# One kernel for two transformer blocks: product tiles completed in pairs around the norms that join the blocks, the two norms made in one step, and one count read of TensorE moved

## The chip, the cores and the metric

The kernel runs on 1 core of one Trainium2 chip. The metric is the time of one execution on the device, in microseconds. TensorE (PE in the profile) multiplies into eight PSUM banks of 128x512 fp32, and loads the stationary operand beside that (PEld); VectorE (DVE), ScalarE (ACT), GpSimd (POOL) and SyncE (SP, which here only issues transfers) work beside it, each through its own instructions in order. Engines wait for each other by semaphores that count up.

## What is computed

Two blocks run one after the other on 512 tokens of width 1024, all in fp32. Only their joint matters here: the end of the first block, the first block's last norm, the second block's first norm, and the product behind it.

```python
def rmsnorm(x, g):
    y = xf * lax.rsqrt(jnp.mean(xf * xf, axis=-1, keepdims=True) + EPS)
    return y.astype(x.dtype) * g
# end of first_block
    x = x + hier_moe(h, w_grp[i], w_exp[i], w1[i], w3[i], w2[i])
    h = rmsnorm(x, g_ple[i])
    x = x + jax.nn.sigmoid(h @ w_pg[i]) * (p[i] @ w_ple[i])
    return rmsnorm(x, g_final)
# start of second_block
    h = rms_norm(x, norm_mix[layer])
    proj = h @ w_in[layer]
```

EPS is 1e-6. The residual x of the second block is the output of the norm by g_final.

## The kernel before

**Products.** Every large product is made of fp32 operands that are each cut into a high part (a rounded fp32r copy, made by ACT: `split_hi` for weights, `act_hi` for activations) and the rest (made by DVE: `split_lo`, `act_lo`). A product of 512 contraction rows by 512 columns is a *chunk*; for each of its 4 token tiles, `tile_passes` issues 4 x 3 matmuls (high x high, high x low, low x high; 12 in all) into the PSUM bank of that tile, `gb[j]`. A *unit* is 512 output columns and has two chunks (kc 0 and 1), so it has 8 tiles of 12 matmuls. Weights of a chunk go through `w_stage[s]`, `w_hi[s]` and `w_lo[s]`, s = 0 or 1 by turns; a slot can be refilled when the last tile that reads it is done (`pe_tiles`).

**The end of block one.** The gate product `g_pg` (h @ w_pg) has two units of 8 tiles. In both, PE takes kc 0 for token tiles 0 to 3, then kc 1 for 0 to 3, so a bank is complete only from the fifth tile on. As a bank completes, ACT makes the sigmoid out of it (`gate_rows`, `sg_t`), and DVE multiplies and adds it into x (`embed`, lines 1717 and 1719; semaphore `x_ple`). The second unit is `second_unit(g_pg)`.

**The two norms.** When a token tile of x is whole, ACT squares and sums its row (`sum_squares`, line 793) and takes the root (line 795); DVE inverts that and scales x by it and g_final in place (`scale_rows`, lines 1283 and 1287). Then the same again for the second block's norm: sum, root, inverse, and the scaled rows go to `xn`. PE turns the scaled rows (`turn_rows`, line 2016, 8 transposes of 128x128 to a token tile), ACT and DVE cut them into `act_hi` and `act_lo` (lines 810 and 1274), and `norm_and_product(4, g_sv)` runs the first product of block two, one unit of 8 tiles. Weights' cuts for `g_sv` stand among these steps (`mid=`).

**Behind it.** A small product with 16 weight columns (line 2447, `low_hi`, `low_lo`) and then `g_gv`. GpSimd clears `low_f` once x is whole, and only then does SP load it, and behind it on the same queue the weights of `g_gv`.

**The count read.** Block one's experts run in rounds of 64 slots. After the first round each engine reads the fullest expert's count (`value_load(most)`; for PE line 2403) and branches over the further rounds (line 2404). With these inputs no further round runs. Behind the branch PE takes the embedding product p @ w_ple (`embedding_tile`, line 2421).

## Time and profile before

| | us |
|---|---|
| runs of the kernel before (3), median | 1835.64 |
| lowest and highest | 1835.12, 1837.38 |
| the profiled execution, whole | 1835.13 |
| its span, first to last instruction | 1833.5 |
| PE busy | 1769.7 |
| DVE, ACT, POOL busy | 796.7, 587.2, 66.3 |

All times of single instructions count from the start of the span. The whole time is 1.6 us more than the span. PE is busy 97% of the span, so what can be won lies in the few places where it stands idle or at half clock, and the mean busy share doesn't show where these are; the chain of waits and the timeline do.

### The profile page before, as it was taken

The page shows a single profiled execution, that of the slowest core. Times are in us where ns is not written, and L with a number is a line of the kernel's source. Part 1 is how long each engine was busy: PE and PEld are TensorE (multiplying, and loading weights), DVE is VectorE, ACT ScalarE, POOL GpSimd, SP SyncE. Part 2 cuts the span into 40 slices and gives each one's busy share as a digit, 9 for nine tenths or more (in the row PEclk, how much of TensorE's full clock was granted, in tenths as well). Part 3 has the DMA queues.
Part 4 walks back from the last instruction along what each step waited for, and adds up shares of the span by engine and source line. Part 5 has one row for each costly group of instructions (what it writes and reads, how often), then busy time and mean ns, then how long its engine had stood idle before and what let it go on. Part 6 is the DMA issues. An engine that isn't in the chain of part 4 may idle for free.

```text
span 1833.5 us, 21542 instructions
## 1 busy us (share of the span) xinstructions
PE 1769.7 (97%) x8428; PEld 1284.1 (70%) x8428; DVE 796.7 (43%) x1104; ACT 587.2 (32%) x729; POOL 66.3 (4%) x123
## 2 busy tenths in 40 slices
PE   6999999979999999999979999999999989999998
PEld 5887887754444454544758777788868878888886
DVE  5323338453333333333553445666656444323432
ACT  5333443222121212122443433344442333213422
POOL 2000000000000000000000012300000000000000
PEclk9999999989999999999989999999999999999999
DMA  5222223947999999999222222223243322233222
GB/s 195 92 92 92 69 69 92 359 167 308 420 421 422 421 417 410 418 409 353 74 64 82 83 93 70 69 76 109 92 139 111 107 69 92 93 108 97 92 92 80
DMA packets 90447, 326.20 MB, mean 178 GB/s; under 512 B 8569, under 2 KB 9089, under 8 KB 65809
## 3 DMA queue, kind: packets, MB, share of 16 engines
q1 hardware_dynamic: 88640, 320.08, 46.6%
q0 software_dynamic: 1744, 5.26, 0.8%
q8 instruction: 43, 0.70, 0.2%
q14 instruction: 20, 0.16, 0.0%
HBM read 319.03 MB, written 6.29 MB: 177 GB/s over the span
## 4 chain that ended last, share of the span: by engine, by line
PE 94%; DVE 3%; ACT 2%; DMA 1%; issue 1%; SPq 0%; DVEq 0%; ACTq 0%
PE bank L1991 59%; PE bank L2303 12%; PE bank L2316 6%; PE bank L2220 3%; PE bank L2263 3%; PE bank L2016 2%; PE bank L2529 2%; ACT xg L957 1%; PE bank L2421 1%; PE bank L2467 1%; PE bank L2488 1%; DMA w_stage<-in_w_in 1%; DVE xn L1287 0%; PE bank L2566 0%; DVE act_lo L1274 0%
## 5 line engine op out<-in xcount | busy, mean ns | idle before, releaser
L1991 PE MATMUL bank<-act_hi,w_hi 128*128 128x512 f32 x992 | 392.0, 395 | 2.0 <-DVE act_lo L1274 2.0
L1259 DVE TENSOR_TENSOR w_lo<-w_stage,w_hi 128x2048 fp32r<-128x2048 f32 x99 | 226.5, 2288 | 378.0 <-ACT w_hi L777 378.0
L1991 PE MATMUL bank<-act_lo,w_hi 128*128 128x512 f32 x992 | 387.8, 391 | 0.0
L1991 PE MATMUL bank<-act_hi,w_lo 128*128 128x512 f32 x992 | 387.8, 391 | 0.0
L777 ACT ACTIVATE w_hi<-w_stage 128x2048 fp32r<-128x2048 f32 x99 | 189.7, 1916 | 415.7 <-PE bank L1991 412.2
L1991 PEld LDWEIGHTS bank<-act_hi,w_hi 128*128 128x128 f32 x992 | 187.4, 189 | 43.9 <-issue 5.9
L2303 PE MATMUL bank<-ring,xgT 128*64 128x512 f32 x992 | 215.7, 592 | 0.7 <-ACT xgT L961 0.7
L1991 PEld LDWEIGHTS bank<-act_hi,w_lo 128*128 128x128 f32 x992 | 187.2, 189 | 39.4
L1991 PEld LDWEIGHTS bank<-act_lo,w_hi 128*128 128x128 f32 x992 | 187.4, 189 | 38.3 <-issue 0.5
L2303 PEld LDWEIGHTS bank<-ring,xgT 128*64 128x64 f32 x992 | 71.1, 137 | 141.6 <-issue 140.6
L1991 PE MATMUL bank<-w_hi,act_hi 128*128 128x512 f32 x288 | 114.2, 397 | 6.0 <-DVE act_lo L1274 5.1
L2316 PE MATMUL bank<-ring,gatedT 128*64 128x512 f32 x512 | 113.4, 595 | 0.8 <-DVE gatedT L1619 0.8
L1991 PE MATMUL bank<-w_hi,act_lo 128*128 128x512 f32 x288 | 113.1, 393 | 0.0
L1991 PE MATMUL bank<-w_lo,act_hi 128*128 128x512 f32 x288 | 113.0, 393 | 0.0
L1991 PE MATMUL bank<-w_hi,hid_hi 128*128 128x512 f32 x256 | 99.6, 389 | 0.0
L1991 PE MATMUL bank<-w_lo,hid_hi 128*128 128x512 f32 x256 | 99.6, 389 | 0.0
L1991 PE MATMUL bank<-w_hi,hid_lo 128*128 128x512 f32 x256 | 99.6, 389 | 0.0
L957 ACT ACTIVATE xg<-bank 128x512 f32<-128x512 f32 x32 | 34.2, 1074 | 191.2 <-PE bank L2220 191.2
L2316 PEld LDWEIGHTS bank<-ring,gatedT 128*64 128x64 f32 x512 | 35.4, 137 | 67.5 <-issue 66.5
L1588 DVE TENSOR_TENSOR x_tm<-x_tm,bank 128x512 f32<-128x512 f32 x128 | 78.0, 680 | 0.0
L1610 DVE TENSOR_TENSOR gated<-gated,bank 128x512 f32<-128x512 f32 x16 | 11.0, 688 | 151.1 <-PE bank L2303 151.1
L1626 DVE SCALAR_TENSOR_TENSOR y_lo_sb<-bank,slot_gate,y_hi_sb 128x512 fp32r<-128x512 f32 x32 | 23.3, 750 | 122.0 <-ACT y_hi_sb L989 121.9
(364 smaller groups left out, 2076.1 us busy)
## 6 DMA issues: line engine op xcount, KB each, us to landing
ring<-in_w SPq DMA_DIRECT2D x188, 1024.0 KB, 11.4
w_stage<-in_w_in SPq DMA_DIRECT2D x46, 1024.0 KB, 5.1
w_stage<-in_w_ff SPq DMA_DIRECT2D x32, 1024.0 KB, 5.2
w_stage<-in_w_out SPq DMA_DIRECT2D x8, 1024.0 KB, 5.1
extra<-in_w SPq DMA_DIRECT2D x4, 1024.0 KB, 7.8
branch_gates<-gate_out POOLq DMA_DIRECT2D x16, 256.0 KB, 2.4
w_stage<-in_w_proj_gla SPq DMA_DIRECT2D x4, 1024.0 KB, 10.0
w_stage<-in_w_pg SPq DMA_DIRECT2D x3, 1024.0 KB, 5.8
```

Of the source, the lines that this page charges most:

```text
L777: act.activation(w_hi[s][:, 0:ktiles, :], w_stage[s][:, 0:ktiles, :], ACT.Copy)\
L957: act.activation(xg_by_row[:, b * (P // 2):(b + 1) * (P // 2), :], mb[b][:, :].rearrange("s (q k) -> s q k", k=KT), ACT.Copy).then_inc(xg_ ...
L1259: dve.tensor_tensor(w_lo[s][:, 0:ktiles, :], w_stage[s][:, 0:ktiles, :], w_hi[s][:, 0:ktiles, :].bitcast(F32), ALU.subtract).then_inc(w_lo ...
L1588: dve.tensor_tensor(xt, xt, bank[:, :], ALU.add).then_inc(moe_added, 1)
L1626: dve.scalar_tensor_tensor(y_lo_sb[:, half], gb[1 + b][:, :], slot_gate[:, col(i)], y_hi_sb[:, half].bitcast(F32), ALU.mult, ALU.subtract)\
L1991: ins = pe.matmul(gb[j][:, :], left, right, start=(kc == 0 and k == 0 and n_pass == 0), stop=(kc == g.chunks - 1 and k == g.ktiles - 1 and ...
L2016: return pe.transpose(dst, src, ident[0:rows, 0:rows])
L2220: return pe.matmul(mb[b][:, :], sel[:, t, :], part[:, t, b * 512:(b + 1) * 512], start=(part is xn_hi and t == 0), stop=(part is xn_lo and ...
L2263: ins = pe.matmul(bank[:, :], selT[:, t * P:(t + 1) * P], part[:, half], start=(part is y_hi_sb), stop=(part is y_lo_sb))
L2303: ins = pe.matmul(dst[mine, :], xgT[:, 4 * kh + k, mine], weights[:, k, :], start=(kh == 0 and k == 0), stop=(kh == 1 and k == 3), skip_gr ...
L2316: return pe.matmul(gb[1 + nh][mine, :], gatedT[:, k, mine], ring[8 + 2 * (k // 2) + q][:, 2 * (k % 2) + nh, :], start=(k == 0), stop=(k == ...
L2529: ins = pe.matmul(mb[t][:, h * P:(h + 1) * P], left[:, h, cols], right[:, h, cols], start=True, stop=True, skip_group_check=True)
```

## The change

1. **Order of tiles.** The second unit of `g_pg` and the unit of `g_sv` take their tiles as PAIRED says: (tile, kc) = 0/0, 1/0, 0/1, 1/1, 2/0, 3/0, 2/1, 3/1. Banks 0 and 1 are complete after the fourth tile. The transposes of token tiles 0 and 1 stand ahead of the last two tiles of `g_pg`, those of 2 and 3 ahead of the fourth and fifth tile of `g_sv`. `split_hi` has a mode `paired` that waits for the sixth tile of a unit and not for all.
2. **The norms.** With m the mean of x squared and q the mean of (x g_final) squared, the two roots in a row are 1/sqrt(q + EPS m + EPS squared). DVE makes `xg_tm` = x g_final by half rows (`final_gain`), ACT sums the squares of x and of xg by half rows, GpSimd makes the joint root of a token tile in three steps (`both_rstd`), and DVE makes xn in one step (`both_norms`). The residual x = xg / sqrt(m + EPS) is made later by ACT (4 instructions of 128x1024), with a root for all tiles from GpSimd.
3. **ACT's table.** A dummy sigmoid stands ahead of the gates; no square root is taken at the joint any more.
4. **The count read.** PE's `value_load` stands in `last_pair` between `turn_gated` and the wait for `gatedT_out`; the branch stays where it was.

```diff
         def rows_count(n, t):
-            if n in (3, 4):
-                return 3 * NT + ((1, 2, 4, 6) if n == 3 else (3, 5, 7, 8))[t]
             return n * NT + t + 1
+        PAIRED = ((0, 0), (1, 0), (0, 1), (1, 1), (2, 0), (3, 0), (2, 1), (3, 1))
...
-            pool.wait_ge(x_ple, 2 * NT)
+            pool.wait_ge(n_sd, rows_count(3, NT - 1))
+            own.did(pool.tensor_scalar(both_var[:, :], ms_x[:, 0, :], EPS, EPS * EPS, ALU.mult, ALU.add))
+            own.settle()
+            own.did(pool.tensor_tensor(both_var[:, :], both_var[:, :], ms_xg[:, 0, :], ALU.add))
+            for t in range(NT):
+                mine = slice(t, t + 1)
+                pool.wait_ge(n_sd, rows_count(4, t))
+                own.settle()
+                own.did(pool.tensor_scalar(both_var[:, mine], ms_x[:, 1, mine], EPS, both_var[:, mine],
+                                           ALU.mult, ALU.add))
+                own.settle()
+                own.did(pool.tensor_tensor(both_var[:, mine], both_var[:, mine], ms_xg[:, 1, mine], ALU.add))
+                own.settle()
+                pool.tensor_tensor(both_rstd[:, mine], both_var[:, mine], root_power[:, mine], ALU.pow)\
+                    .then_inc(pg_scale, 1)
+            own.did(pool.tensor_tensor(row_rstd[:, :], ms_x[:, 0, :], ms_x[:, 1, :], ALU.add))
+            own.settle()
+            own.did(pool.tensor_scalar(row_rstd[:, :], row_rstd[:, :], EPS, None, ALU.add))
+            own.settle()
+            pool.tensor_tensor(row_rstd[:, :], row_rstd[:, :], root_power[:, :], ALU.pow).then_inc(pg_scale, 1)
+            pool.wait_ge(x_ple, 3 * NT)
             pool.memset(low_f[:, :, :], 0.0).then_inc(low_pad, 1)
...
-                if not isinstance(c, int) or c >= 2:
+                if paired:
+                    act.wait_ge(pe_tiles, (c - 1) * 4 + 2)
+                elif not isinstance(c, int) or c >= 2:
...
+            act.activation(table_col[:, :], one_col[:, :], ACT.Sigmoid)
+            def gate_rows(u, j, before):
+                act.wait_ge(pe_tiles, (g_pg.chunk0 + 2 * u) * 4 + before)
+                if u:
+                    act.wait_ge(x_ple, j + 1)
+                act.activation(sg_t[j][:, :], gb[j][:, :], ACT.Sigmoid, scale=rstd[:, j:j + 1]).then_inc(out_act, 1)
+            def row_squares(rows, u, t, sums, junk):
+                half = slice(u * 512, (u + 1) * 512)
+                return act.activation(junk[:, t, half], rows[:, t, half], ACT.Square, scale=float(D) ** -0.5,
+                                      accum_out=sums[:, u, t:t + 1])
+            def squares_x(u, t):
+                act.wait_ge(x_ple, NT + 2 * t + 1 if u else t + 1)
+                row_squares(x, u, t, ms_x, sq_tm)
+            def squares_xg(u, t):
+                if u:
+                    act.wait_ge(x_ple, NT + 2 * t + 2)
+                else:
+                    act.wait_ge(n_xn, rows_count(3, t))
+                row_squares(xg_tm, u, t, ms_xg, xn_at[4]).then_inc(n_sd, 1)
+            def rows_high(t):
+                for b in range(2):
+                    q = 2 * t + b
+                    act.wait_ge(n_tp, turned_before(4) + q + 1)
+                    act.activation(act_hi[:, 4 * b:4 * b + 4, t * P:(t + 1) * P],
+                                   mb[q % 4][:, :].rearrange("p (k t) -> p k t", k=4), ACT.Copy).then_inc(n_hi, 1)
             split_hi(g_pg.chunk0 + 2, 0)
             act.wait_ge(pg_scale, 1)
-            gate_rows(0)
+            for j in range(4):
+                gate_rows(0, j, 4 + j + 1)
             split_hi(g_pg.chunk0 + 3, 1)
-            gate_rows(1)
-            def end_of_block(t):
-                act.wait_ge(x_ple, NT + t + 1)
-                sum_squares(3, t)
-            def next_rows(t):
-                if t + 1 < NT:
-                    end_of_block(t + 1)
-                act.wait_ge(n_xn, rows_count(3, t))
-            end_of_block(0)
-            norm(4, next_rows, mid=lambda: split_hi(g_sv.chunk0, 0))
+            for t in range(NT):
+                squares_x(0, t)
+                squares_xg(0, t)
+            for t in range(2):
+                gate_rows(1, t, 3 + t)
+                squares_x(1, t)
+                squares_xg(1, t)
+            split_hi(g_sv.chunk0, 0, paired=True)
+            rows_high(0)
+            gate_rows(1, 2, 7)
+            rows_high(1)
+            gate_rows(1, 3, 8)
             split_hi(g_sv.chunk0 + 1, 1)
+            for t in range(2, NT):
+                squares_x(1, t)
+                squares_xg(1, t)
+            rows_high(2)
+            rows_high(3)
+            act.wait_ge(pg_scale, 2 + NT)
+            for t in range(NT):
+                own.did(act.activation(x[:, t, :], xg_tm[:, t, :], ACT.Copy, scale=row_rstd[:, t:t + 1]))
...
+            def final_gain(u, j):
+                half = slice(u * 512, (u + 1) * 512)
+                if u == j == 0:
+                    dve.wait_ge(gain_in, 48)
+                dve.wait_ge(x_ple, NT + 2 * j + 1 if u else j + 1)
+                dve.tensor_tensor(xg_tm[:, j, half], x[:, j, half], gain[:, half], ALU.mult)\
+                    .then_inc(x_ple if u else n_xn, 1)
+            def both_norms(t):
+                if t == 0:
+                    dve.wait_ge(gain_4_in, 16)
+                dve.wait_ge(pg_scale, t + 2)
+                dve.scalar_tensor_tensor(xn_at[4][:, t, :], xg_tm[:, t, :], both_rstd[:, t:t + 1], gain_4[:, :],
+                                         ALU.mult, ALU.mult).then_inc(n_xn, 1)
+            def rows_low(t):
+                for b in range(2):
+                    q = 2 * t + b
+                    dve.wait_ge(n_hi, turned_before(4) + q + 1)
+                    rest(act_lo[:, 4 * b:4 * b + 4, t * P:(t + 1) * P],
+                         mb[q % 4][:, :].rearrange("p (k t) -> p k t", k=4),
+                         act_hi[:, 4 * b:4 * b + 4, t * P:(t + 1) * P]).then_inc(n_lo, 1)
             for j in range(NT):
                 embed(0, j)
+                final_gain(0, j)
             split_lo(g_pg.chunk0 + 3, 1)
-            def end_of_block(t):
-                if t + 1 < NT:
-                    embed(1, t + 1)
-                scale_rows(3, t)
-            embed(1, 0)
-            norm(4, end_of_block, mid=lambda: split_lo(g_sv.chunk0, 0))
+            for t in range(2):
+                embed(1, t)
+                final_gain(1, t)
+            both_norms(0)
+            both_norms(1)
+            split_lo(g_sv.chunk0, 0)
+            rows_low(0)
+            rows_low(1)
+            embed(1, 2)
             split_lo(g_sv.chunk0 + 1, 1)
+            final_gain(1, 2)
+            embed(1, 3)
+            final_gain(1, 3)
+            both_norms(2)
+            both_norms(3)
+            rows_low(2)
+            rows_low(3)
...
+            def paired_unit(g, u, before={}):
+                for n, (j, kc) in enumerate(PAIRED):
+                    if n in before:
+                        before[n]()
+                    tile_passes(g, g.chunk0 + 2 * u + kc, g.tile0 + 4 * u + j, kc, kc, j, fm=False)
...
                     turn_gated(n)
+                    if r is None:
+                        counts.append(pe.value_load(most[0:1, 0:1], min_val=0, max_val=T))
                     pe.wait_ge(gatedT_out, n + 1)
...
+            counts = []
             experts_pe(None)
-            fullest = pe.value_load(most[0:1, 0:1], min_val=0, max_val=T)
+            fullest = counts[0]
...
-            second_unit(g_pg)
-            norm_and_product(4, g_sv)
+            paired_unit(g_pg, 1, {6: lambda: turn_rows(4, 0), 7: lambda: turn_rows(4, 1)})
+            def rows_split(q):
+                pe.wait_ge(n_lo, turned_before(4) + q + 1)
+            def turned_and_split(t, q):
+                turn_rows(4, t)
+                rows_split(q)
+            paired_unit(g_sv, 0, {0: lambda: rows_split(0), 1: lambda: rows_split(2), 2: lambda: rows_split(3),
+                                  3: lambda: turn_rows(4, 2), 4: lambda: turned_and_split(3, 4),
+                                  5: lambda: rows_split(6), 6: lambda: rows_split(7)})
```

What the order of instructions shows at three places (names carry buffer numbers; `xn` is the scaled rows, `bank4` and up are the banks for transposes).

PE, the joint, before: the last matmuls of `g_pg`'s second unit, then the transposes of token tiles 0 and 1 and the first tile of `g_sv`.

```order
L1991 MATMUL bank3<-w_hi1_86,act_hi_81 128x512
L1991 MATMUL bank3<-w_lo1_88,act_hi_81 128x512
L1991 MATMUL bank3<-w_hi1_86,act_lo_82 128x512
L2016 MATMUL bank4<-ident_50,xn_2_91 128x128 x4
L2016 MATMUL bank5<-ident_50,xn_2_91 128x128 x4
L2016 MATMUL bank6<-ident_50,xn_2_91 128x128 x4
L2016 MATMUL bank7<-ident_50,xn_2_91 128x128 x4
L1991 MATMUL bank0<-w_hi0_85,act_hi_81 128x512
```

And now, behind the sixth tile of that unit:

```order
L2082 MATMUL bank3<-w_hi0_86,act_hi_82 128x512
L2082 MATMUL bank3<-w_lo0_88,act_hi_82 128x512
L2082 MATMUL bank3<-w_hi0_86,act_lo_83 128x512
L2107 MATMUL bank4<-ident_50,xn_2_92 128x128 x4
L2107 MATMUL bank5<-ident_50,xn_2_92 128x128 x4
L2082 MATMUL bank2<-w_hi1_87,act_hi_82 128x512
L2082 MATMUL bank2<-w_lo1_89,act_hi_82 128x512
```

The first transposes moved from behind the unit to ahead of its last two tiles (bank 2 and bank 3 with `w_hi1`).

DVE, the joint, before: adds into x, the two norms in turn, and the weight cut of `g_sv`'s first chunk.

```order
L1717 TENSOR_TENSOR ple_tm<-ple_tm,sg_t_172 128x512
L1719 TENSOR_TENSOR x_tm<-x_tm,ple_tm 128x512
L1283 RECIPROCAL rstd<-rstd 128x1
L1287 SCALAR_TENSOR_TENSOR x_tm<-x_tm,rstd,gain 128x1024
L1717 TENSOR_TENSOR ple_tm<-ple_tm,sg_t_173 128x512
L1719 TENSOR_TENSOR x_tm<-x_tm,ple_tm 128x512
L1283 RECIPROCAL rstd<-rstd 128x1
L1287 SCALAR_TENSOR_TENSOR x_tm<-x_tm,rstd,gain 128x1024
L1283 RECIPROCAL rstd<-rstd 128x1
L1287 SCALAR_TENSOR_TENSOR xn_91<-x_tm,rstd,gain_94 128x1024
```

And now, from the add of token tile 1 to that of token tile 3:

```order
L1778 TENSOR_TENSOR x_tm<-x_tm,ple_tm 128x512
L1786 TENSOR_TENSOR xg_tm<-x_tm,gain 128x512
L1794 SCALAR_TENSOR_TENSOR xn_92<-xg_tm,row_sums,gain_95 128x1024 x2
L1318 TENSOR_TENSOR w_lo_88<-w_stage_84,w_hi_86 128x2048
L1333 TENSOR_TENSOR act_lo<-bank,act_hi 128x4x128 x4
L1776 TENSOR_TENSOR ple_tm<-ple_tm,sg_t_175 128x512
L1778 TENSOR_TENSOR x_tm<-x_tm,ple_tm 128x512
L1318 TENSOR_TENSOR w_lo_89<-w_stage_85,w_hi_87 128x2048
L1786 TENSOR_TENSOR xg_tm<-x_tm,gain 128x512
L1776 TENSOR_TENSOR ple_tm<-ple_tm,sg_t_176 128x512
```

Tiles 0 and 1 are normed, the first weight cut and their `act_lo` are done before tile 2 is added; the second weight cut now stands between the add of tile 2 and its product with g_final.

PE, the end of the experts, before: the last spread matmuls, the count read and the branch.

```order
L2263 MATMUL bank<-y_hi_sb,selT 128x512
L2263 MATMUL bank<-y_lo_sb,selT 128x512
L2403 TENSOR_LOAD most
L2403 ISA x2
L2404 COMPARE_AND_BRANCH
```

And now, where the count is read:

```order
L2107 MATMUL bank<-ident,gated 128x128 x4
L2475 TENSOR_LOAD most
L2475 ISA x2
L2414 MATMUL bank<-ring_128,gatedT 64x512
L2414 MATMUL bank<-ring_129,gatedT 64x512
```

The read stands some 48 matmuls earlier; only the compare and branch is left behind the spreads.

## Rows read from the trace of the kernel before

**Rows 1.** The page, busy time, share of the span and instructions of PE and others.

```profile
PE 1769.7 (97%) x8428; PEld 1284.1 (70%) x8428; DVE 796.7 (43%) x1104; ACT 587.2 (32%) x729; POOL 66.3 (4%) x123
```

**Rows 2.** Stretches: length, busy PE, PEld, DVE, ACT, POOL; granted clock, DMA share, GB/s.

```profile
884.00:886.00 2.00, 2.00 (x7) 1.53 (x6) 2.00 (x3) 0.60 (x1) 0.00 (x0) 0.50 0.00 0
899.00:943.00 44.00, 43.98 (x196) 36.12 (x194) 16.43 (x17) 16.95 (x22) 1.29 (x2) 1.00 0.28 96
943.00:960.00 17.00, 4.32 (x17) 3.52 (x18) 13.27 (x19) 15.26 (x28) 0.95 (x1) 0.57 0.08 9
1326.00:1328.00 2.00, 2.00 (x10) 1.77 (x11) 1.93 (x4) 2.00 (x5) 0.00 (x0) 1.00 0.00 0
```

**Rows 3.** Chain of waits in order of time: start us, us, what.

```profile
899.43 43.56 PE bank L1991 x192
...
963.95 0.87 PE bank L2016 x8
...
984.80 5.44 PE bank L2447 x24
```

**Rows 4.** Timeline of PE at the joint: start, us, instruction, idle before.

```profile
942.59 0.39 PE L1991 MATMUL bank<-w_hi,act_lo 128*128 128x512 f32 x1
952.10 1.97 PE L2016 MATMUL bank<-ident,xn 128*128 128x128 f32 x8 [9.12 <-DVE xn L1287]
...
959.62 0.80 PE L1991 MATMUL bank<-w_hi,act_hi 128*128 128x512 f32 x1 [1.43 <-DVE act_lo L1274]
```

**Rows 5.** PE's sequencer, lines 2403 and 2404: duration ns, start us.

```profile
L2403 PEldq TENSOR_LOAD <-most x1: 488/488/488, 878.4 to 878.4; - x1
L2404 PEldq COMPARE_BRANCH  x1: 3671/3671/3671, 879.3 to 879.3; - x1
```

**Rows 6.** Timeline of PE after two other idle stretches.

```profile
883.11 0.47 PE L2421 MATMUL bank<-ple_hi,pT_hi 128*128 128x512 f32 x1 [2.51 <-DVE x_tm L1588]
...
884.23 0.63 PE L2421 MATMUL bank<-ple_lo,pT_hi 128*128 128x512 f32 x1
...
886.79 0.63 PE L2421 MATMUL bank<-ple_lo,pT_hi 128*128 128x512 f32 x1
...
1325.92 4.37 PE L2544 MATMUL bank<-gv_tm,gkend_tm 128*128 128x256 f32 x19 [1.71 <-ACT gkend_tm L1175]
```

**Rows 7.** Timeline of ACT around the second unit of g_pg.

```profile
903.93 1.06 ACT L1036 ACTIVATE sq_tm<-x_tm 128x1024 f32<-128x1024 f32 x1
...
921.26 0.69 ACT L1045 ACTIVATE sg_t<-bank,rstd 128x512 f32<-128x512 f32 x1 [2.03 <-PE bank L1991]
921.84 1.91 ACT L777 ACTIVATE w_hi<-w_stage 128x2048 fp32r<-128x2048 f32 x1
...
943.02 0.69 ACT L1045 ACTIVATE sg_t<-bank,rstd 128x512 f32<-128x512 f32 x1 [2.03 <-PE bank L1991]
...
953.88 1.06 ACT L810 ACTIVATE act_hi<-bank 128x512 fp32r<-128x512 f32 x2
```

**Rows 8.** Timeline of DVE, the same stretch.

```profile
921.98 0.69 DVE L1717 TENSOR_TENSOR ple_tm<-ple_tm,sg_t 128x512 f32<-128x512 f32 x1 [1.30 <-ACT sg_t L1045]
...
923.79 2.29 DVE L1259 TENSOR_TENSOR w_lo<-w_stage,w_hi 128x2048 fp32r<-128x2048 f32 x1 [0.39 <-ACT w_hi L777]
...
950.76 1.28 DVE L1287 SCALAR_TENSOR_TENSOR xn<-x_tm,rstd,gain 128x1024 f32<-128x1024 f32 x1
...
958.29 1.28 DVE L1274 TENSOR_TENSOR act_lo<-bank,act_hi 128x512 fp32r<-128x512 f32 x2
```

**Rows 9.** Timeline of POOL: the root of norm 2.

```profile
906.21 0.24 POOL L725 TENSOR_SCALAR ssq<-ssq 128x4 f32<-128x4 f32 x1 [650.35 <-ACT sq_tm L1036]
906.54 1.05 POOL L727 TENSOR_TENSOR rstd<-ssq,root_power 128x4 f32<-128x4 f32 x1
```

**Rows 10.** Instructions of POOL's line 744: ns min/median/max, first and last start.

```profile
L744 POOL TENSOR_SCALAR_AFFINE_SELECT sb_w<-sb_w x32: 287/541/1207, 1078.7 to 1186.7; 128x128 f32<-128x128 f32 x32
```

**Rows 11.** DMA issues from 900 to 1000 us: KB each, median us to landing.

```profile
w_stage<-in_w_in SPq DMA_DIRECT2D x6, 1024.0 KB, 5.0
```

More of the change, by code:

```diff
@@ L281, in two_blocks @@
         gain_2 = at("gain_2", F + 0, [P, D])
+        xg_tm = at("xg_tm", F + 8, [P, NT, D])
         pg_stage = at("pg_stage", F + 4, [P, 4, 512])
@@ L1037, in _ @@
                                accum_out=ssq[:, t:t + 1]).then_inc(n_sd, 1)
-            def gate_rows(u):
-                for j in range(4):
-                    act.wait_ge(pe_tiles, (g_pg.chunk0 + 2 * u + 1) * 4 + j + 1)
-                    if u:
-                        act.wait_ge(x_ple, j + 1)
-                    act.activation(sg_t[j][:, :], gb[j][:, :], ACT.Sigmoid, scale=rstd[:, j:j + 1]).then_inc(out_act, 1)
+            act.activation(table_col[:, :], one_col[:, :], ACT.Sigmoid)
[4 more added lines that the diff above has]
+                act.activation(sg_t[j][:, :], gb[j][:, :], ACT.Sigmoid, scale=rstd[:, j:j + 1]).then_inc(out_act, 1)
@@ L1067, in _, with unit @@
+            act.wait_ge(pg_scale, 2 + NT)
+            for t in range(NT):
+                own.did(act.activation(x[:, t, :], xg_tm[:, t, :], ACT.Copy, scale=row_rstd[:, t:t + 1]))
             act.wait_ge(low_in, 32)
             act.activation(low_hi[:, :, :], low_f[:, :, :], ACT.Copy).then_inc(low_split, 1)
-            def unit(c, put, next_two=True):
-                split_hi(c + 2, 0)
+            def unit(c, put, next_two=True, paired=False):
+                split_hi(c + 2, 0, paired=paired)
@@ L1075, in unit @@
                     split_hi(c + 3, 1)
-            unit(g_sv.chunk0, evac_f(sbv, ACT.Copy))
+            own.settle()
+            unit(g_sv.chunk0, evac_f(sbv, ACT.Copy), paired=True)
             act.wait_ge(low_z, 1)
```

6 lines of the change are left out of this document (5 added, 1 removed).

## The prediction

> **What bounds the kernel now.** I read the page first: PE is busy for 1769.7 us, 97% of the span [rows 1]. So only places where PE stands idle or runs at half clock can give time back. The stretches show where: from 899 to 943 us, the gate product, PE is full and the granted clock is 1.00; from 943 to 960 us PE is busy for 4.32 of 17 us at a mean clock of 0.57 [rows 2]. The timeline of PE shows the same place: its last matmul of the gate product ends at 942.98, the first transposes start at 952.10 after 9.12 us idle, and the product of block two starts at 959.62 [rows 4]. The chain of waits says what the stretch costs: the next product of PE, line 2447, starts at 984.80, and what had to be done between is 96 matmuls and 4 turned token tiles. At full clock a matmul takes 43.56/192 = 0.227 us and a turned tile 0.87 us [rows 3], so the work is 96 x 0.227 + 4 x 0.87 = 25.3 us, out of 984.80 - 942.98 = 41.8. The joint loses 16.5 us; that is the ceiling of what parts 1 to 3 of the change can bring.
>
> A second, smaller gap lies ahead of the embedding product: PE idle for 2.51 us before 883.11, then matmuls of 0.63 us instead of 0.39; the first of these is at 884.23 and the seventh at 886.79, so 0.43 us apart instead of 0.227 [rows 6]. The granted clock there was 0.50, which is 1.2 GHz [rows 2]. With the one that the clock's fall met half way I count 8 slow matmuls: the stretch costs 8 x 0.2 = 1.6 us.
>
> **The change, part by part.** I keep the times of the trace before, and put the shift from the count read on at the end. A tile is 12 matmuls, 2.72 us. A gate starts on ACT 0.04 us after its tile; the last did at 943.02, so the k-th tile of the second unit frees its gate at 943.02 - (16 - k) x 2.72, counting the first unit's eight tiles as 1 to 8.
>
> *First unit and the weights behind it.* The gain product adds a DVE step of 0.69 us to each token tile. The last gate is at 921.26 [rows 7]; the two steps of its add follow from 921.98 on [rows 8], to 923.40, and the gain product to 924.1; the weight cut behind it moves from 923.79 [rows 8] to about 924.1 and ends at 926.4 instead of 926.1. In the new order PE wants it two tiles sooner, for tile 11, at about 926.5. It fits with 0.1 us left, and I cost it at nothing; if it is late, it is late by tenths.
>
> *Squares.* The 8 half squares of the first unit's columns are ACT's while PE works. For one I estimate 1.06 us less 0.43 for half the columns (the 2048-column copy takes 1.91, the 1024-column square 1.06 [rows 7]), so 0.63: 5 us from 923.8, done ahead of the first gate at 929.4. They are hidden.
>
> *Token tiles 0 and 1.* Bank 0 is complete at tile 11: gate 929.42, add done 931.55, gain product 932.3, its squares 932.95, and gate 1 only then (932.95, not 932.14, since ACT takes its work in order). Gain product 1 ends at 935.8, its squares at 936.5. The root on GpSimd is three steps: 0.24, about 0.24, and 1.05 for the power [rows 9], with gaps of 0.1: 1.8 us. Root 0 is there at 934.8, root 1 at 938.3. DVE's joint norm of tile 0 takes 1.28 us (the step of the same form [rows 8]): 935.8 to 937.1. PE wants it at 937.4. Norm 1 ends at 939.6, wanted at 937.4 + 0.87 + 2.72 = 941.0. No stall.
>
> *Weights and low parts of g_sv.* Its first high cut starts when tile 14 is done, 937.6, and takes 1.91; the low cut 939.6 to 941.9; `act_lo` of token tile 0 to 943.1 [rows 7, 8]. PE wants all that at 942.98 + 2 x 0.87 - 0.2 = 944.5. The second high cut follows the last gate (944.76): 945.35 to 947.3, the low cut to 949.6, wanted two tiles in, at 950.0. Both fit, the second with 0.4 us left.
>
> *Token tiles 2 and 3.* Here is the one stall that I expect. DVE stands at the second weight cut until 949.6; behind it are the gain product of tile 2 (950.2), whose squares end at 950.85. Root 2 is there at 952.65 if GpSimd takes 1.8 us, and norm 2 at 953.95. PE wants it after the third tile of g_sv, at 944.55 + 3 x 2.72 = 952.7: 1.25 us of stall. GpSimd's price is the term that the trace does not show: its rows for the power were measured beside an idle DVE. For a form that GpSimd ran 32 times beside a busy DVE the row has 287 ns at least, 541 in the middle and 1207 at most [rows 10]. That bounds what a held step adds: 0 or 0.92 us each, so the stall is 1.25 to 4.0 us. During root 2 DVE runs four steps of two SBUF operands nearly without a gap, so I take the middle row, 0.25 us for each of three steps: a stall of 2.0. Root 3 is wanted 3.6 us after root 2's norm is taken, and ready in time.
>
> The Trainium skill (GPSIMD Engine Reference, Key points) says that GpSimd shares its SBUF interfaces with VectorE and contends with its instructions of two SBUF inputs; embed and the gain product are of that kind. The page gives no price; by it the stall would lie above 1.25, as in my sum and, further, in the rival of the held steps.
>
> *Behind the product.* GpSimd clears low_f now behind all its roots, at about 957.7 (before: as soon as x was whole), and SP's transfers of g_gv's weights stand behind that clearing: issue near 959.5, landed 5.0 us later [rows 11], cut by ACT and DVE by 969.5. PE wants them behind line 2447, at 970.2 + 5.44 = 975.7. The four scalings that make x (about 1.1 us each, estimated from the 1.06 of the 1024-column square) end at 964 to 965, low_hi and low_lo by 967.5, wanted at 970.2. All hidden, with 2.7 us left at the least; the old cover was longer.
>
> *Sum of the joint.* 4 x 0.87 + 96 x 0.227 + 2.0 = 27.3 us in place of 41.8: 14.5 to 14.6 us won. The clock: an idle stretch of 1.71 us was followed by 1.00 [rows 2, 6], one of 2.51 by 0.50. I take it that 2.0 us does not lower it; if it does, it costs a slow stretch like that one, 1.6 us.
>
> *Count read.* The load starts at 878.4 and the branch at 879.3: 0.9 us, and then the branch takes 3.67 [rows 5], which is why PE waits until 883.1. The new place is ahead of a wait for a copy on DVE in which PE is idle anyway, so the 0.9 us is hidden there, by a margin of a few tenths. The branch starts 0.9 earlier and the idle stretch shrinks from 2.51 to 1.6 us, below the 1.71 after which the clock held; then the slow stretch behind it is gone too, 1.6 us. From there on every start is PE's (the copies and cuts of that stage wait for it), so both reach the end: 2.5 us.
>
> The Trainium skill (Runtime: NRT & Kernel Launch, Instruction fetch mechanics) says that a taken branch to a target outside the fetched pages stalls for a transfer of the page. By that rule the stall moves with the branch, which agrees with my sum and speaks against the rival in which the read brings nothing.
>
> Sum: 14.6 + 2.5 = 17.1 us. From the profiled execution's 1835.13 that gives 1818.0; this execution lies 0.5 us below the median of the runs shown and at their lower end, so the median may come out some tenths higher.
>
> **Rivals.**
> - *A shorter stall, or none,* is inside the forecast: without any the time would be 1816.0.
> - *GpSimd's steps are held hard.* At the top row of 1207 ns the stall at token tile 2 is 4.0 us, and the clock then falls for one stretch: 2.0 + 1.6 more, 1821.6. For it: DVE is dense exactly there. Against: the middle row is less than half of the top.
> - *The count read brings nothing.* If the branch waits until PE has run its queue empty (880.6), it ends where it did, the idle stretch and the half clock stay: 1835.13 - 14.6 = 1820.5. For it: the branch ends 2.4 us after the queue is empty, a figure that could be its own. Against: its row starts at 879.3, behind the load, and the load alone stands between it and the last matmul issued.
> - *Another operand is late at several tiles*, the two weight cuts with 0.1 and 0.4 us left: each 0.1 us more on ACT or DVE goes straight to PE. At 1 to 2 us for each cut and with the held roots the time is 1823 to 1827.
> - *Slower than before:* the first turn stalls PE, the clock falls to 1.2 GHz and does not come back until the product ends, since transposes and short waits stand between its tiles. Each tile would cost 12 x 0.2 = 2.4 us more; ten tiles 24 us: 1842. It decides from 7 slow tiles on. Against: the clock that was 0.50 at 884 to 886 was 1.00 all through 899 to 943 [rows 2], though transposes stand between the embedding's tiles too.
>
> **How the numbers follow.** Forecast 1818.0 (its own range 1816 to 1820): 0.58. Held roots: 0.17. Count read worth nothing: 0.12. Late operands: 0.09. Slower: 0.02; no effect, the gain eaten by waits that I do not see: 0.02. The range reaches from 1815.5 (no stall, less the scatter of half a microsecond) to 1823.5, which takes in held steps or a worthless count read, each alone, nearly both together (1824.1), and the smaller half of the late operands. A measurement here can tell 0.2%, 3.7 us, from no change. All cases but the last two are faster by more than that: faster 0.96, same 0.02, slower 0.02.
>
> **What would show it.** PE idle between the first transposes and line 2447 of 1 to 2.5 us in one piece, ahead of the turn of token tile 2; granted clock 1.00 over that stretch; from the last tile of the first gate unit to line 2447's start 21.8 + 27.3 = 49 us instead of 63.6. GpSimd's three steps by their rows: 1.8 us in all or 2.5. PE's idle before the embedding product 1.6 us and its matmuls 0.39. Wrong would be the step on which a stall stands ahead of tile 11, of g_sv's first or third tile, or of line 2447.

## The result and the profile after

| | before | after |
|---|---|---|
| median of 4 runs each, us | 1836.29 | 1819.05 |
| lowest and highest | 1835.12, 1837.38 | 1818.27, 1820.32 |
| the profiled execution | 1835.13 | 1818.27 |
| its span | 1833.5 | 1816.5 |

The ratio is 0.9907, with a 95% interval of 0.9890 to 0.9924: 17.2 us faster, where 17.1 were forecast. Below, a kernel is compared by four stretches between starts of PE's pieces in the chain of waits: **A** from the last down product to the embedding product, **B** from there to the gate product's second half by line 2082 (1991 before), **C** from there to the small product of line 2557 (2447 before), which holds the joint, and **D** from there to the end of the span. What lies ahead of A isn't touched by any edit, except that the moved read now stands at its end.

The page of the changed kernel, parts 1 and 2, says only that PE has 4.8 us less busy time than before [rows 1], which fits some 5 us of matmuls and transposes at half clock that are gone from B and C, and GpSimd 9 us more:

```profile
span 1816.5 us, 21572 instructions
PE 1764.9 (97%) x8428; PEld 1280.5 (70%) x8428; DVE 796.5 (44%) x1100; ACT 589.4 (32%) x741; POOL 75.7 (4%) x140
```

The chain of waits of the changed kernel, from stretch A to the end of C (start, duration, what):

```profile
869.70 7.11 PE bank L2414 x32
...
882.48 5.71 PE bank L2522 x24
...
897.23 38.12 PE bank L2082 x168
935.35 0.87 PE bank L2107 x8
936.23 2.77 PE bank L2082 x12
939.00 0.87 PE bank L2107 x8
939.87 2.75 PE bank L2082 x12
...
942.64 0.02 ACT sg_t L1073
942.67 0.56 issue
943.23 1.92 ACT w_hi L805
945.15 0.02 issue
945.17 2.29 DVE w_lo L1318
947.46 0.61 DVE xg_tm L1786
...
948.10 0.73 ACT xn L1077 x2
...
948.92 0.61 POOL row_sums L743
...
950.82 1.29 DVE xn L1794
...
952.16 1.09 PE bank L2107 x8
...
956.90 10.89 PE bank L2082 x48
967.79 5.44 PE bank L2557 x24
```

PE's tiles run through: 168 matmuls without a break, the transposes of token tiles 0 and 1 between tiles. The chain leaves PE once, from 942.6 on, through ACT's gate and second weight cut, DVE's second weight cut, the gain product behind it, the squares, the root and the norm of token tile 2. That is the path on which the prediction put the stall. The timeline of PE gives its size and that of the idle stretch ahead of the embedding product:

```profile
882.48 0.47 PE L2522 MATMUL bank<-ple_hi,pT_hi 128*128 128x512 f32 x1 [1.83 <-DVE x_tm L1647]
952.16 1.09 PE L2107 MATMUL bank<-ident,xn 128*128 128x128 f32 x8 [1.40 <-DVE xn L1794]
```

The windows of the changed kernel (width, then busy time of PE, PEld, DVE, ACT and POOL, granted clock, DMA) show that neither costs clock. In the stretch in which it was 0.50 [rows 2] it is now 1.00, which is the level of 2.4 GHz, and so is it all over the joint:

```profile
884.00:886.00 2.00, 2.00 (x11) 1.65 (x10) 2.00 (x3) 1.09 (x2) 0.00 (x0) 1.00 0.00 0
940.00:975.00 35.00, 33.60 (x157) 27.73 (x156) 19.13 (x20) 19.60 (x28) 6.96 (x10) 1.00 0.32 100
```

From the starts in the chains [rows 3], with these two of the kernel before,

```profile
869.63 7.11 PE bank L2316 x32
...
883.12 7.31 PE bank L2421 x24
```

A went from 13.49 to 12.78 us, B from 16.31 to 14.75, C from 85.37 to 70.56, and D is 848.7 in both. So 0.7 us came from the moved read, 1.6 from the clock that no longer falls behind it, and 14.8 from the joint. In its new place the read costs nothing: PE is idle ahead of the last down product for 0.78 us with it and for 0.79 without.

### The profile page after: what moved, and what is told of

The parts are those of the page before. It is cut to its first block, busy times and chain, and to the rows that moved or that the text cites. A ratio compares the mean times of both kernels' runs of the same rounds, so it can differ in the third digit from the quotient of the medians.

```text
span 1816.5 us, 21572 instructions
## 1 busy us (share of the span) xinstructions
PE 1764.9 (97%) x8428; PEld 1280.5 (70%) x8428; DVE 796.5 (44%) x1100; ACT 589.4 (32%) x741; POOL 75.7 (4%) x140
## 4 chain that ended last, share of the span: by engine, by line
PE 94%; DVE 2%; ACT 2%; DMA 1%; issue 0%; POOL 0%; SPq 0%; DVEq 0%; POOLq 0%; ACTq 0%
PE bank L2082 59%; PE bank L2401 12%; PE bank L2414 6%; PE bank L2318 3%; PE bank L2361 3%; PE bank L2107 2%; PE bank L2639 2%; ACT xg L985 1%; PE bank L2577 1%; PE bank L2522 1%; PE bank L2598 1%; DMA w_stage<-in_w_in 1%; PE bank L2676 0%; PE bank L2665 0%; DVE w_lo L1318 0%
```

## The experiments

Two theories stood against each other for each part. **Joint:** the gain comes from order and joint norm together, each of which alone leaves other stalls; the rival is that one of them carries it and the other is idle. **Remaining stall:** DVE's order and steps on GpSimd held by VectorE; the rival is ACT or transfers. **Count read:** the load is hidden while the branch keeps its price; the rival is that the branch waits for PE's empty queue. All stretches, in us from the profiled execution of each kernel; "ahead" is the time from the start of the span to A:

| kernel | median us (runs) | ahead | A | B | C | D |
|---|---|---|---|---|---|---|
| before | 1836.29 (4) | 869.6 | 13.49 | 16.31 | 85.37 | 848.7 |
| after | 1819.05 (4) | 869.7 | 12.78 | 14.75 | 70.56 | 848.7 |
| after_again | 1819.26 (4) | 869.8 | 12.48 | 14.72 | 70.59 | 848.8 |
| count_only | 1832.25 (12) | 869.8 | 12.51 | 14.76 | 86.55 | 844.4 |
| count_back | 1820.46 (6) | 872.2 | 13.25 | 16.38 | 70.58 | 844.5 |
| norms_only | 1822.65 (5) | 869.2 | 12.70 | 14.76 | 74.08 | 848.7 |
| order_only | 1824.16 (6) | 870.9 | 13.51 | 16.37 | 75.24 | 848.4 |
| gain_first | 1819.03 (5) | 871.1 | 12.42 | 14.75 | 69.68 | 849.6 |
| gain_first_again | 1814.63 (4) | 871.3 | 12.46 | 14.75 | 69.70 | 849.4 |
| pool_beside_sbuf | 1820.01 (1) | 871.7 | 12.62 | 14.76 | 70.58 | 848.6 |
| pool_beside_psum | 1818.52 (1) | 869.7 | 12.40 | 14.76 | 70.58 | 849.3 |
| no_branch | 1819.17 (4) | 871.8 | 10.97 | 14.49 | 70.56 | 847.1 |
| small_body | 1816.61 (1) | 871.8 | 10.97 | 14.45 | 70.58 | 847.1 |
| mid_body | 1815.75 (1) | 870.9 | 10.97 | 14.48 | 70.60 | 847.0 |

### The count read alone, and put back

count_only is the kernel before with this edit; count_back is the changed kernel with it undone.

```diff
                     turn_gated(n)
+                    if r is None:
+                        counts.append(pe.value_load(most[0:1, 0:1], min_val=0, max_val=T))
                     pe.wait_ge(gatedT_out, n + 1)
...
+            counts = []
             experts_pe(None)
-            fullest = pe.value_load(most[0:1, 0:1], min_val=0, max_val=T)
+            fullest = counts[0]
```

> The kernel before with nothing changed but the place of PE's count read. Theory (the read is 0.9 us in front of the branch, and the shorter idle stretch keeps the clock up): PE's branch starts 0.8 to 0.9 us earlier, PE idle ahead of the embedding product is 1.8 us instead of 2.51, granted clock 1.00 from 884 to 886 us instead of 0.50, and 2.0 to 2.5 us off the time. Rival (the branch alone decides, it waits until PE's queue is empty): no change, idle 2.5 us, clock 0.50, ratio 1.000. A third outcome would be the 0.6 us without the clock.

> The changed kernel with the count read put back in front of the branch, all else kept. Theory: idle ahead of the embedding product 2.5 us again, half clock behind it, and 2.2 us more than the changed kernel's 1819.05 (span 1818.7 to 1819.0 instead of 1816.5); the joint itself unchanged at 70.6 us from the gate product's start to line 2557. Rival (the parts are not independent; the clock phase decides and not the length of the idle stretch): clock stays at 1.00 and only 0.6 us are lost.

Measured: 1832.25 us (ratio to before 0.9984, interval 0.9975 to 0.9994) and 1820.46 (0.9921, 0.9908 to 0.9934). Over all profiles A is 12.4 to 12.8 us with the read moved and 13.25 to 13.51 without, B 14.7 against 16.3 to 16.4. The two effects in A and B are the same in the old kernel and in the new one. The rival in which the branch decides alone and the read brings nothing falls. In count_only C is 1.2 us longer than before, though nothing in it was edited: PE's idle stretches in the joint are the same to 0.01 us, but all 12 matmuls of the first tile behind them run at half clock (5.46 us) where about half of them did before (4.33). With the read put back, PE's timeline and windows show what B pays:

```profile
885.45 0.47 PE L2519 MATMUL bank<-ple_hi,pT_hi 128*128 128x512 f32 x1 [2.28 <-DVE x_tm L1647]
...
886.82 0.63 PE L2519 MATMUL bank<-ple_hi,pT_lo 128*128 128x512 f32 x1
887.25 0.63 PE L2519 MATMUL bank<-ple_hi,pT_hi 128*128 128x512 f32 x1
```

```profile
886.80:890.20 3.40, 3.40 (x10) 2.65 (x9) 3.40 (x3) 0.75 (x2) 0.00 (x0) 0.54 0.00 0
```

2.28 us of idle time instead of 1.83, and 3.4 us at a granted clock of 0.54 follow. The medians say less than the stretches: count_only's is 4.0 us below that of before (by its ratio it is 2.9), where A and B give 2.5 and C takes back 1.2, and count_back's is 1.4 us above that of the changed kernel, where A and B give 2.1. The stretches that nobody edited scatter by more than such differences (below).

### One half of the joint's change at a time

norms_only keeps the joint norm and puts the tiles back into the old order; order_only pairs the tiles and makes the two norms in turn. Only the cores of the edits:

```diff
# norms_only, against the changed kernel
-            paired_unit(g_pg, 1, {6: lambda: turn_rows(4, 0), 7: lambda: turn_rows(4, 1)})
...
+            second_unit(g_pg)
+            norm_and_product(4, g_sv)
# order_only, against the kernel before
-                return 3 * NT + ((1, 2, 4, 6) if n == 3 else (3, 5, 7, 8))[t]
+                return 3 * NT + ((1, 2, 5, 6) if n == 3 else (3, 4, 7, 8))[t]
...
+            def both_scales(a, b):
+                for n in (3, 4):
+                    for t in (a, b):
+                        scale_rows(n, t)
```

> The changed kernel with the old order of tiles in both units and the old place of the transposes; the norms are still one step, and ACT and DVE take the rows in an order fit for that. Theory (both parts are needed: the last banks complete only at the unit's end, so token tile 0's row sums, root, norm, transposes and low parts come partly behind it): PE stalls of about 3 to 5 us in all at the joint, 1 to 4 us slower than the changed kernel, 1820 to 1823. Rival (the pairing is the whole gain and the joint root is idle talk): 8 us or more slower than the changed kernel, near 1828 or above.

> The kernel before with the pairs of tiles and the new places of the transposes, but with the two norms in turn as before (squares, root on ACT, inverse and scaling on DVE, twice); count read as before. Theory (the chain of a token tile through two norms is about 6 us plus table loads, against 3.7 us through the joint one): stalls at the turn of tile 0 (2 to 4 us) and of tile 2 (3 to 5 us), so 5 to 8 us of the joint's 16.5 remain lost; 1826 to 1829. Rival (pairing is the whole gain): within 1 us of the changed kernel plus the count read, 1820 to 1822.

Measured: 1822.65 us (0.9932, 0.9919 to 0.9945) and 1824.16 (0.9935, 0.9921 to 0.9950). By C the joint norm alone wins 11.3 of the 14.8 us and the paired order alone 10.1. Together that would be 21.4: both take the same 16.5 us that the joint lost, and neither alone gets all. For the joint norm the nearer comparison is count_only, which has the read moved too: 86.55 - 74.08 = 12.5 us. order_only came out faster than I had expected (1824.16 where 1826 to 1829 stood): its second stall is 1.62 us and not 3 to 5. What each leaves is a wait of 2.7 us ahead of a turn, and half clock behind it. PE's timeline and window of norms_only:

```profile
944.47 1.54 PE L2106 MATMUL bank<-ident,xn 128*128 128x128 f32 x8 [2.70 <-DVE xn L1797]
...
946.26 0.63 PE L2081 MATMUL bank<-w_lo,act_hi 128*128 128x512 f32 x1
```

```profile
945.00:949.00 4.00, 4.00 (x15) 3.28 (x13) 3.93 (x7) 3.22 (x7) 1.92 (x4) 0.58 0.01 2
```

and of order_only, whose second wait stands at token tile 2:

```profile
941.53 1.09 PE L2046 MATMUL bank<-ident,xn 128*128 128x128 f32 x8 [2.67 <-DVE xn L1302]
...
960.37 1.09 PE L2046 MATMUL bank<-ident,xn 128*128 128x128 f32 x8 [1.62 <-DVE xn L1302]
```

Behind the 2.67 us of order_only the next tile takes 4.35 us instead of 2.75, behind its 1.62 us it takes 2.75. The rival that one half carries it and the other is idle falls. How much each half gets alone belongs to the order in which ACT and DVE were put for it; other orders weren't run.

### Token tile 2's gain product ahead of the weight cut

```diff
             embed(1, 2)
-            split_lo(g_sv.chunk0 + 1, 1)
             final_gain(1, 2)
+            split_lo(g_sv.chunk0 + 1, 1)
```

> The changed kernel with DVE's product of token tile 2 with g_final moved ahead of the second weight cut of g_sv. Theory (the one stall that is left, 1.4 us ahead of the turn of token tile 2, comes from DVE standing at that weight cut with the gain product behind it): root 2 is ready by 948 us, the stall falls to 0 to 0.3 us, 1.1 to 1.4 us off the changed kernel's time. Rival (the stall comes from GpSimd's held steps or from DVE's amount of work): the stall stays above 1 us, time unchanged.

> Token tile 2's gain product ahead of g_sv's second weight cut, once more beside the changed kernel. By its joint stage (69.7 against 70.56 us) it should be 0.9 us shorter; if the scatter of the granted clock in other stages (2 to 3 us from run to run) is as large as it was, the two medians lie within 1.5 us of each other in either order, and the joint's stage alone tells them apart, again by 0.8 to 0.95 us.

> The changed kernel once more, to be compared with the next one on the same chip: 1817.5 to 1820.5 us, the joint's stage 70.5 to 70.6 us, the embedding's stage 14.75 us with the clock held.

The stall went from 1.40 to 0.53 us and C from 70.56 to 69.68, both times (69.70 beside 70.59): 0.9 us, less than the 1.1 to 1.4 expected. GpSimd took back the rest. Its timeline and DVE's in gain_first:

```profile
947.47 1.66 POOL L743 TENSOR_SCALAR row_sums<-row_sums 128x1 f32<-128x1 f32 x1 [10.62 <-ACT xn L1077]
949.21 0.64 POOL L746 TENSOR_TENSOR row_sums<-row_sums 128x1 f32<-128x1 f32 x1
949.93 1.00 POOL L748 TENSOR_TENSOR row_sums<-row_sums,root_power 128x1 f32<-128x1 f32 x1
```

```profile
946.18 2.29 DVE L1318 TENSOR_TENSOR w_lo<-w_stage,w_hi 128x2048 fp32r<-128x2048 f32 x1 [1.04 <-ACT w_hi L805]
948.39 0.69 DVE L1776 TENSOR_TENSOR ple_tm<-ple_tm,sg_t 128x512 f32<-128x512 f32 x1
949.11 0.69 DVE L1778 TENSOR_TENSOR x_tm<-x_tm,ple_tm 128x512 f32<-128x512 f32 x1
```

The first step starts beside the weight cut and goes on through the step behind it, which follows without a gap; it ends at 949.13, 0.05 us behind that step's end at 949.08. Then DVE is free for 0.03 us. The second ends at 949.85, 0.05 behind 949.80. The root took 3.46 us instead of 1.87: by the gate product's start, which is 1.01 us later here, it was ready 0.87 us earlier than in the changed kernel, and not by 948 as expected.

The medians don't agree with each other: 1819.03, then 1814.63, where the changed kernel beside it has 1819.26. I had expected the two within 1.5 us; they were 4.6 apart. All nine runs of gain_first have the median 1817.00 (1812.32 to 1821.17), the eight of the changed kernel 1819.05 (1817.73 to 1820.72). By the medians it is the fastest complete kernel here; 0.9 us of that is shown by C, the rest isn't shown to come from the edit.

### What holds a step on GpSimd

Two kernels put more work for DVE between norm 0 and norm 1, beside GpSimd's root 1: one step with two SBUF operands, or two with a PSUM operand. The results go to a spare tile that nobody reads.

```diff
             both_norms(0)
+            dve.tensor_tensor(spare[:, :], gain[:, :], gain_4[:, :], ALU.mult)        # pool_beside_sbuf
+            for b in range(2):                                                        # pool_beside_psum
+                dve.tensor_copy(spare[:, b * 512:(b + 1) * 512], mb[2 + b][:, :])
             both_norms(1)
```

> The changed kernel with one added DVE product of two SBUF operands (128x1024, into a spare buffer) between the joint norms of token tiles 0 and 1, beside GpSimd's root of tile 1. Theory (a step of GpSimd that starts beside a DVE step of two SBUF operands ends only when that step ends): one of the three root steps grows from 0.19 or 0.55 us until about 0.1 us behind the added product's end, so the root is there at 936.6 us instead of 935.8. Rival (the longer steps are chance or belong to GpSimd alone): the three steps keep 0.47, 0.19 and 0.55 us.

> The same, but what DVE does beside the root of token tile 1 is two copies of 128x512 out of PSUM, about as long. Theory (it is the two SBUF operands that hold GpSimd): the steps beside the copies keep 0.19 and 0.55 us and the root is there at 935.8. Rival (any DVE work holds GpSimd): a step grows to the end of the copies, as with the SBUF product.

The timelines of GpSimd and DVE with the two SBUF operands, 1820.01 us:

```profile
936.35 1.52 POOL L744 TENSOR_SCALAR row_sums<-row_sums 128x1 f32<-128x1 f32 x1 [1.90 <-ACT xn L1078]
937.96 0.19 POOL L747 TENSOR_TENSOR row_sums<-row_sums 128x1 f32<-128x1 f32 x1
```

```profile
936.61 1.22 DVE L1814 TENSOR_TENSOR spare<-gain,gain 128x1024 f32<-128x1024 f32 x1
```

and with the PSUM operands, 1818.52 us (one run each):

```profile
934.15 0.47 POOL L744 TENSOR_SCALAR row_sums<-row_sums 128x1 f32<-128x1 f32 x1 [1.91 <-ACT xn L1078]
934.70 0.19 POOL L747 TENSOR_TENSOR row_sums<-row_sums 128x1 f32<-128x1 f32 x1
934.97 0.56 POOL L749 TENSOR_TENSOR row_sums<-row_sums,root_power 128x1 f32<-128x1 f32 x1
```

```profile
934.40 1.28 DVE L1815 COPY spare<-bank 128x512 f32<-128x512 f32 x2
```

GpSimd's step starts at 936.35, beside the end of norm 0, which the added step follows without a gap. DVE's added step ends at 937.83 and GpSimd's at 937.87, 1.52 us long. Beside the copies, from 934.40 to 935.68, GpSimd's steps take 0.19 and 0.56 us, as with DVE idle; the 0.47 ahead of them stood beside norm 0, itself a step of two SBUF operands. The two added pieces of work differ in two things, the number of operands and where they lie. One more row helps: in the changed kernel the power of all four tiles stands beside DVE's `act_lo`, one PSUM and one SBUF operand, and takes 1.04 us, as beside an idle DVE (1.05 [rows 9]). A DVE step with one SBUF operand and nothing else wasn't run. C stays at 70.58 in both, as the root of token tile 1 has time. The Trainium skill (GPSIMD Engine Reference, Key points) says that the two engines contend for SBUF interfaces when VectorE has two SBUF inputs; the runs agree. Their price here: a step of GpSimd lasts until the step of DVE beside it is over, and through the next one where DVE goes on without a gap.

### PE's branch

no_branch takes PE's branch out of the changed kernel, small_body and mid_body leave it and shrink what it skips. All three leave out PE's further rounds, which these inputs don't enter.

```diff
             with pe.If(fullest > SLOTS):
                 with pe.Fori(1, ROUNDS) as r:
                     with pe.If(fullest > r * SLOTS):
-                        experts_pe(r)
-                        pe.wait_ge(moe_added, r * (8 * PAIRS) + 8 * PAIRS)
+                        for _ in range(64):                    # mid_body; small_body: nothing
+                            pe.matmul(gb[0][:, :], pT_hi[:, 0, 0:P], ple_hi[:, 0, 0:512], start=True, stop=True)
                         pe.sem_inc(wait_carrier, 1)
```

> The changed kernel without PE's branch and without PE's part of the further rounds, which these inputs do not reach; the other engines keep theirs. Theory (the 3.8 us of the branch are the fetch of its target, and they stand on PE's path): PE starts the embedding product when its queue is free, near 880.6 us and at the latest 881.5, instead of 882.48, so 1.0 to 1.9 us off the changed kernel, if DVE's rows (first one ready near 884.4) do not become the limit. Rival (PE waits for the adds of the experts anyway): start stays at 882.4.

> The changed kernel, in which the body that PE would branch over (its further rounds, not run with these inputs) holds a single semaphore increment in place of a round of the experts; PE's further rounds are left out. Theory A: the 3.4 to 3.8 us of PE's compare-and-branch are those of going on at a place far from the instructions at hand. Then a near target costs at most 0.3 us, the embedding product follows the last spreads without idle, and the two stages before the gate product's second half take 10.9 to 11.3 and 14.4 to 14.8 us, as without a branch. Theory B: it is the price of any taken branch after a register read on PE. Then the branch's row stays at 3.3 to 3.9 us and the stages at 12.4 to 12.8 and 14.75 us.

> The same with 64 matmuls in the body that is branched over (they are not run; PE's further rounds are left out). Theory A: 64 instructions are still a jump out of what lies at hand or not, which sets it near 0.3 us or near 3.5 us, a step and not a price per instruction: a price in proportion to the skipped code would be well under 0.5 us for a body some twenty times shorter. Theory B: 3.3 to 3.9 us as ever.

The rows of line 2505 on PE's sequencer (duration, then start), first of the changed kernel, then of small_body, then of mid_body:

```profile
L2505 PEldq COMPARE_BRANCH  x1: 3844/3844/3844, 878.5 to 878.5; - x1
```

```profile
L2505 PEldq COMPARE_BRANCH  x1: 208/208/208, 880.6 to 880.6; - x1
```

```profile
L2505 PEldq COMPARE_BRANCH  x1: 367/367/367, 879.7 to 879.7; - x1
```

Without the branch, or over a short body, A is 10.97 us in all three and the embedding product follows the spreads without idle time. So the whole of PE's wait ahead of it, 1.4 to 1.8 us, is the branch, and what the branch costs hangs on what it skips. B is 0.3 us shorter as well. no_branch's median shows nothing of these 2.1 us (1819.17 beside 1819.05); its profiled execution, 1816.70 us, lies 1.6 us below the changed kernel's. The profile put that wait down to DVE's x_tm; DVE does the same adds in small_body and PE waits for none. The Trainium skill (Runtime: NRT & Kernel Launch, Instruction fetch mechanics) has a taken branch to a target outside the fetched pages stall for a transfer; the runs agree, as theory A did. Theory B, one price for every taken branch behind a register read, falls. Which part of the 3.4 to 3.8 us is that transfer no run shows. The rival of a price for each skipped instruction is weaker, not excluded. From one increment to 64 matmuls the branch rose by 0.16 us; the whole body, counted in the kernel, has 296 matmul calls, whose like leave 448 records in the profile. That is not the twenty times of the expectation but 5 to 7 times 64, so an estimate in proportion is 0.9 to 1.3 us and not 3.4. No body between the two was run. Against a reading by distance alone stands that the same branch takes 54 ns on ACT and 63 on DVE, over bodies of their own.

### Where the scatter of the totals comes from

No experiment touched stretch D, and still it lasts 844.4 to 849.6 us; what lies ahead of A lasts 869.2 to 872.2. In D the windows of the profiles show half clock in two places, in one profile and not in the other. The changed kernel, count_back and gain_first:

```profile
1000.00:1060.00 60.00, 60.00 (x250) 47.55 (x249) 21.44 (x26) 25.01 (x24) 0.00 (x0) 0.97 0.27 88
1440.00:1500.00 60.00, 55.24 (x247) 45.10 (x246) 30.27 (x34) 23.34 (x35) 0.00 (x0) 0.94 0.23 71
```

```profile
1000.00:1060.00 60.00, 60.00 (x258) 47.79 (x257) 21.52 (x27) 26.48 (x25) 0.00 (x0) 1.00 0.26 88
1440.00:1500.00 60.00, 55.24 (x258) 45.42 (x257) 30.27 (x34) 24.16 (x34) 0.00 (x0) 1.00 0.22 71
```

```profile
1440.00:1500.00 60.00, 55.40 (x243) 45.25 (x241) 30.31 (x34) 23.38 (x34) 0.00 (x0) 0.91 0.22 70
```

With 1.00 in both places D is 844.4 to 844.5, with 1.00 and 0.94 (no_branch and the two short bodies) it is 847.0 to 847.1, with 0.97 and 0.94 it is 848.4 to 848.8, and with 0.97 and 0.91 it is 849.3 to 849.6. That orders all fourteen profiles. The matmuls count it: 8 and 11 fewer in the two windows of the changed kernel than in count_back's, at 0.227 us each, are 4.3 us beside 4.2 by D.

What PE does ahead of these places is the same in all, up to where the clock falls. At the first it has no idle time: it runs eight matmuls of 16 contraction rows (3.70 us), and behind them the clock is 0.50 or 1.00. At the second it is idle for 1.30, 1.49 and 1.97 us, with transposes between. Behind that the first matmul of the changed kernel and that of count_back, with the same waits:

```profile
1458.65 0.76 PE L2082 MATMUL bank<-act_hi,w_hi 128*128 128x512 f32 x1 [1.97 <-DVE act_lo L1333]
```

```profile
1461.70 0.47 PE L2082 MATMUL bank<-act_hi,w_hi 128*128 128x512 f32 x1 [1.97 <-DVE act_lo L1333]
```

So a total of a few runs can't tell an edit that is worth 1 us from none, and a stretch of one profile can, if the clock in it is looked at (the 1.2 us of count_only's C were such a case). The two kernels that were profiled twice had the same levels both times, so whether the edit or the single execution sets them isn't known. That executions of one kernel scatter for this reason isn't shown either, though it fits: in gain_first the mean granted clock was 0.994 at 1812.32 us and 0.988 at 1821.17. Why the clock falls in one profile and not in the next stays open.

## Why the prediction was right

- **The joint's ceiling and work.** The forecast was 96 matmuls, 4 turned tiles and one stall in place of 41.8 us, 14.6 us won. Measured: 14.8, and the changed kernel loses nothing in the joint but the stall of 1.40 us and some tenths of first matmuls.
- **No stall at token tiles 0 and 1, none at the weights.** Right. The steps stand where they were put: with the 2.20 us by which the gate product now starts earlier, root 0 was forecast at 932.6 and came at 932.57, norm 1's end at 937.4 and came at 937.16, the first low cut's end at 939.7 (939.69), the second at 947.4 (947.46). The two margins of 0.1 and 0.4 us held. For root 0 two errors cancel: it took 1.62 us where 1.8 stood, since its power, 0.54 us unheld, was held for 0.99 beside DVE's next add.
- **The stall at the turn of token tile 2.** Place and path right, size 1.40 us where 2.0 was taken. The mis-sized term is the root: 1.8 us was forecast unheld and 2.55 held; it is 1.2 unheld (0.27, 0.19 and 0.54 with their gaps), since the power of 128x1 takes 0.54 us where the row used [rows 9] was for 128x4 (1.05, and 1.04 again in the profile after), and 1.87 in place. What holding added is 0.7 us, where 0.75 was forecast, but that is luck: I took the middle of a row of other steps, and the runs show that the price depends on where DVE's step ends. In the changed kernel two steps of GpSimd came late into two steps of 0.69 us. Beside the cut of 2.29 us and the steps behind it, as in gain_first, it is three times as much (3.46 - 1.2).
- **The clock.** "2.0 us of idle does not lower it" was not tested at 2.0. In stretches A to C idle times of 1.40 to 1.83 us that PE met at full clock left it at 1.00, and those of 2.28 to 2.70 were followed by half clock. But the length alone doesn't decide. The trace of before holds a row that the prediction didn't use, at 1475.64: 1.97 us idle, behind 1.30 and 1.50 us shortly before, and its first matmul takes 0.76 us, at half clock; in 12 of the 14 profiles the clock was down there, in two it was not. So with that row the step from 1.71 to 2.0 us was a risk, and the stall of 1.40 us didn't put it to the test. The rival of the hard-held steps would have been right about the clock, had they come.
- **The count read.** 0.9 and 1.6 us were forecast, 0.7 and 1.56 measured here, 0.9 and 1.6 as means over the kernels. The idle stretch itself came out at 1.83 us where 1.6 stood, above the 1.71 that the argument leaned on, and the clock held all the same. The rival in which the branch waits for PE's empty queue falls: with a short body it starts 1.8 us before PE's last matmul of the spreads and takes 0.2 us.
- **Behind the product.** The cover was there: ACT starts the high cut of g_gv's weights at 963.16, 0.48 us after it could, and PE wants them at 973.2.
- **The total.** That 17.1 and 17.2 us lie so near each other is in part luck. The two profiles compared have the same time ahead of A (869.6 and 869.7) and the same D (848.7); between other kernels these differ by up to 3.0 and 5.2 us, more than any term but the joint's.
- **The distance to the median.** The changed kernel's profile, too, lies 0.8 us below its median, as that of before did by 0.5 of the three runs shown then, and by 1.2 of all four.

## What to carry to other kernels

Where two norms in a row stand between products, order of tiles and number of steps eat the same idle time: cost them together, and look at which single step is late when both are in. Read a wait from its path and not from the releaser that the profile names, and judge an edit of a microsecond by the stretch that it touches, with the clock in that stretch, not by the total. Before a step goes to GpSimd, look at what DVE runs beside it: steps of two SBUF operands hold it to their end.

## What I had not expected of the hardware

- A GpSimd step of 0.19 to 0.27 us that starts beside a DVE step of two SBUF operands lasts until that step ends, or the next where there is no gap: 1.66 us at most here, ending 0.04 to 0.14 us behind DVE (the power 0.4). Copies from PSUM hold it by nothing that shows.
- PE's taken branch over its further rounds costs 3.37 to 3.84 us of its sequencer, over 64 matmuls 0.37, over one increment 0.21. Why the same branch is cheap on ACT and DVE wasn't tried.
- The granted clock has low stretches, away from any edit, that are there in one profile and not in another behind the same work and the same waits, and make D 844.4 or 849.6 us.
